# Regrouping the matmuls of each 128 by 128 weight tile: six of 260 columns become five of 280, 480 and 240

## What is computed

```python
xn = _rmsnorm(x, n_mix_pre);  proj = xn @ w_in            # 1024 -> 8192
q, fp, iv, og, lx, ly, ga, gb = jnp.split(proj, idx, axis=-1)
...
o, S_new = _hgrn2(qh, kk, vh, logf, S0, chunk)            # 8 heads, decaying state
out_a = (norm(o) * silu(og)) @ w_pa
h, h_last = _rglru(conv(lx), ...);  out_b = (gelu(ly) * h) @ w_pb
merged = sigmoid(ga) * out_a + sigmoid(gb) * out_b
x = x + _rmsnorm(merged @ w_o, n_mix_post)
gate, up = jnp.split(_rmsnorm(x, n_ffn_pre) @ w_fi, 2, axis=-1)   # 1024 -> 2 x 2816
x = x + _rmsnorm((silu(gate) * up) @ w_fo, n_ffn_post)
```

## Time and profile before

| | |
|---|---|
| three runs, median (lowest to highest) | 1102.22 us (1102.03 to 1102.48) |
| profiled execution, first to last instruction | 1098.3 us |
| its time outside that span | not recorded; the median of the runs is 3.9 us above the span |
| TensorE matmul busy / weight load busy | 96% / 94% |
| DVE busy / ACT busy | 52% / 40% |
| mean granted TensorE clock | 0.992 of 2.4 GHz |
| matmuls, of them by `ktile` (line 1223) | 8542, 7392 |

### The profile page before, as it was taken

The page is one execution under the profiler, slowest core; times in us unless marked ns, Lnnn a source line. Parts: engine busy times, 40 slices in busy tenths (PEclk is TensorE's granted clock), DMA queues, the critical chain, the costliest instruction groups (busy, mean ns, idle before and its releaser), DMA issues.

```text
span 1098.3 us, 21670 instructions
## 1 busy us (share of the span) xinstructions
PE 1055.9 (96%) x8542; PEld 1034.8 (94%) x8542; DVE 573.2 (52%) x1028; ACT 434.1 (40%) x588; POOL 2.9 (0%) x9
## 2 busy tenths in 40 slices
PE   4899999999999999999999999699999999999997
PEld 3799999999999899999999999699999999999997
DVE  2666566657656788833333333855554554422223
ACT  5434335433442888822222233652323232322222
POOL 0000000000000000000000000000000000000000
PEclk9999999999999899999999999899999999999999
DMA  5533223222332233232333244033233323233321
GB/s 155 162 90 99 79 76 98 86 76 76 94 108 60 81 93 86 78 95 81 91 95 95 88 130 135 20 97 95 80 92 95 95 82 90 67 92 94 94 76 78
DMA packets 182881, 100.36 MB, mean 91 GB/s; under 512 B 3709, under 2 KB 181378, under 8 KB 182594
## 3 DMA queue, kind: packets, MB, share of 16 engines
q1 hardware_dynamic: 164898, 90.87, 27.8%
q10 hardware_dynamic: 17792, 8.91, 2.7%
q0 software_dynamic: 160, 0.15, 0.0%
HBM read 90.79 MB, written 9.13 MB: 91 GB/s over the span
## 4 chain that ended last, share of the span: by engine, by line
PE 90%; DVE 3%; ACT 2%; issue 1%; SPq 1%; DMA 1%; DVEq 0%; ACTq 0%
PE proj L1223 78%; PE pr L1322 5%; PE pi L1371 1%; DMA raw<-in_w_in 1%; PE pr L1376 1%; PE pi L1353 1%; PE pr L1345 1%; PE pi L1414 1%; PE pr L1414 1%; PE pi L1359 0%; ACT wh L358 0%; SPq L266 0%; DVE tmp L1122 0%; DVE acts L1110 0%; DVE raw L1202 0%
## 5 line engine op out<-in xcount | busy, mean ns | idle before, releaser
L1223 PE MATMUL proj<-acts,wh 128*128 128x260 f32 x4928 | 810.7, 287 | 15.5 <-DVE acts L1110 9.2
L1223 PEld LDWEIGHTS proj<-acts,wh 128*128 128x128 f32 x4928 | 679.9, 190 | 23.7 <-DVE acts L1110 10.8
L1223 PE MATMUL proj<-acts,wl 128*128 128x260 f32 x2464 | 498.5, 284 | 0.0
L1223 PEld LDWEIGHTS proj<-acts,wl 128*128 128x128 f32 x2464 | 381.9, 190 | 0.0
L720 DVE TENSOR_TENSOR wl<-raw,wh 128x1024 fp32r<-128x1024 f32 (+2 forms) x164 | 190.8, 1163 | 278.7 <-ACT wh L358 278.6
L358 ACT ACTIVATE wh<-raw 128x1024 fp32r<-128x1024 f32 (+2 forms) x164 | 165.6, 1010 | 358.9 <-PE proj L1223 350.5
L1322 PE MATMUL pr<-tmp 128*128 128x64 f32 (+1 forms) x512 | 66.4, 272 | 3.2 <-DVE tmp L947 3.2
L1322 PEld LDWEIGHTS pr<-tmp 128*128 128x128 f32 x512 | 62.9, 192 | 4.0 <-DVE tmp L947 3.4
L805 DVE TENSOR_TENSOR tmp<-tmp 128x256 f32<-128x256 f32 x56 | 23.6, 422 | 25.5 <-PE pr L1322 25.4
L676 ACT ACTIVATE acts<-tmp 128x520 f32 (+1 forms) x21 | 13.4, 639 | 42.4 <-DVE tmp L1170 42.4
L673 ACT ACTIVATE tmp<-tmp 128x520 f32<-128x520 f32 x21 | 13.5, 641 | 40.0 <-DVE tmp L1161 40.0
(11 more groups left out here) (239 smaller groups left out, 721.0 us busy)
## 6 DMA issues: line engine op xcount, KB each, us to landing
raw<-in_w_in SPq DMA_DIRECT2D x64, 512.0 KB, 4.0
raw<-in_w_ffn_in SPq DMA_DIRECT2D x44, 512.0 KB, 3.8
raw<-in_w_ffn_out SPq DMA_DIRECT2D x16, 384.0 KB, 3.1
raw<-in_w_ffn_out SPq DMA_DIRECT2D x16, 320.0 KB, 2.9
tmp<-in_state_hgrn ACTq DMA_DIRECT2D x8, 512.0 KB, 4.1
out<-tmp ACTq DMA_DIRECT2D x8, 512.0 KB, 3.2
raw<-in_w_branch_a SPq DMA_DIRECT2D x8, 512.0 KB, 3.6
raw<-in_w_branch_b SPq DMA_DIRECT2D x8, 512.0 KB, 3.5
```

Source lines behind the costliest of these rows:

```text
L1223: o = mm(pp[par][:, hf, 0:TH], w, x[:, hf * TH:(hf + 1) * TH], start=start and n == 0, stop=stop and n == 2)
```

## The change

In `ktile` the 520 tokens are cut into a front of 280 (`TFR`) and a back of 240 (`TB`). The front, in the first bank, still gets three matmuls, of 280 columns. For the back the activation's high and low rows stand side by side in one access pattern (two runs of 240 columns), so that one matmul with the high weight streams 480 columns into the second bank; a fifth one adds the low weight times the high activation onto the first 240 of them. At the end the second bank holds two blocks of 240 that have to be added: `lift` on ACT copies the second block into SBUF (`FL`), `fold` on DVE adds it onto the first, in PSUM. `lift` stands in front of ACT's `prep` and waits for the end of the unit, `fold` stands in front of DVE's `prep`; consumers now wait for `folded`. In FFO, where four units add up, there is one pair for four units. Since front and folded back are adjacent, `proj(par)` becomes one run of 520 columns. To make room in SBUF the masks are kept once instead of four times and broadcast in `take`; one copy makes them instead of eight. In the last head's part `prep(u0 + 2, 2)` on ACT moves ahead of `pre_conv(0)`.

```diff
+TB = 240
+TFR = T - TB
+PB = 512 - TFR
...
+            def lift(par, units):
+                eng.wait_ge(E("unit_done"), units)
+                act(FL[:, par], PF[par][:, 512 + TB:512 + 2 * TB], AF.Copy).then_inc(E("lifted"), 1)
...
                 if prev:
+                    lift(1, 4 * h)
                     prep(4 * h + 1, 1)
-                    eng.wait_ge(E("unit_done"), 4 * h)
+                    eng.wait_ge(E("folded"), 4 * h)
                     eng.wait_ge(E("d_f"), h)
-                    act(halves(SIG), proj(1), AF.Sigmoid).then_inc(E("a_sg"), 1)
+                    act(SIG, proj(1), AF.Sigmoid).then_inc(E("a_sg"), 1)
...
+            lift(0, u0 + 1)
+            prep(u0 + 2, 2)
             pre_conv(0, u0)
-            prep(u0 + 2, 2)
...
+            def fold(par, units):
+                eng.wait_ge(E("lifted"), units)
+                back = PF[par][:, 512:512 + TB]
+                tt(back, back, FL[:, par], ADD).then_inc(E("folded"), 1)
...
-            for i in range(NLEV):
-                n = P if i == 0 else P // 2
-                at = 0 if i == 0 else P + (i - 1) * n
-                src = raw[:, 3].rearrange("p k n -> p (k n)")[:, at:at + n].unsqueeze(1).to_broadcast([P, NCH, n])
-                cp(mask(i).rearrange("p (c n) -> p c n", c=NCH), src).then_inc(E("m_made"), 1)
+            cp(masks[:], raw[:, 3].rearrange("p k n -> p (k n)")[:, 0:MW]).then_inc(E("m_made"), 1)
...
                 if prev:
+                    fold(1, 4 * h)
                     prep(4 * h + 1, 1)
                     level(h - 1, 4)
...
-                xh, xl = acts[:, reg[0] + koff + k], acts[:, reg[1] + koff + k]
+                ih, il = reg[0] + koff + k, reg[1] + koff + k
+                xh, xl = acts[:, ih], acts[:, il]
+                both = acts[:, bass.ds(ih, 2, step=il - ih), TFR:T]
                 a, b = wh[:, s % 2, k, :], wl[:, s % 2, k, :]
-                for n, (w, x) in enumerate(((a, xh), (a, xl), (b, xh))):
-                    for hf in range(2):
-                        o = mm(pp[par][:, hf, 0:TH], w, x[:, hf * TH:(hf + 1) * TH],
-                               start=start and n == 0, stop=stop and n == 2)
+                front, back = PF[par][:, PB:512], PF[par][:, 512:512 + TB]
+                mm(front, a, xh[:, 0:TFR], start=start, stop=False)
+                mm(front, a, xl[:, 0:TFR], start=False, stop=False)
+                mm(front, b, xh[:, 0:TFR], start=False, stop=stop)
+                mm(PF[par][:, 512:512 + 2 * TB], a, both, start=start, stop=False, skip_group_check=True)
+                o = mm(back, b, xh[:, TFR:T], start=False, stop=stop, skip_group_check=True)
```

More of the change, by code:

```diff
@@ L135, in hybrid_decoder @@
         cout = sb("cout", [P, 3 * (1 + NB), NH])
+        FL = sb("lifts", [P, 2, TB])
         pp = [ctx.enter_context(nc.psum_tensor(f"proj{i}", [P, 2, 512], F32)) for i in range(2)]
+        PF = [t[:].rearrange("p a n -> p (a n)") for t in pp]
         pr = ctx.enter_context(nc.psum_tensor("pr", [P, 2, 512], F32))
@@ L195, in mask @@
         def mask(i):
-            return masks[:, 0:TP] if i == 0 else masks[:, TP + (i - 1) * TP // 2:TP + i * TP // 2]
+            return masks[:, 0:P] if i == 0 else masks[:, P + (i - 1) * P // 2:P + i * P // 2]
         NX = CW - 1 + T + CW * NB
@@ L566, in _ @@
             eng.wait_ge(E("p_os"), NH)
+            lift(1, u0 + 2)
             squares_of_ly(0)
@@ L573, in _ @@
             out_high(h)
+            lift(0, u0 + 3)
             pre_conv(1, u0 + 2)
@@ L583, in _ @@
                     n = i * 2 + bb
+                    lift(1, u0 + 2 * bb)
                     squares_of_ly(n - 1)
@@ L588, in _ @@
                     gates(n - 1)
+                    lift(0, u0 + 2 * bb + 1)
                     prep(u0 + 2 * bb + 2, (2 * bb + 2) % 4)
@@ L593, in _ @@
                 ch.end(Q_LRU - 1)
+            lift(1, 4 * G_MIX)
             squares_of_ly(NH - 1)
@@ L598, in _ @@
             gates(NH - 1)
+            lift(0, 4 * G_MIX + 1)
             prep(4 * G_MIX + 2, 2)
@@ L654, in _ @@
                     turned_x1(j - 1)
+            lift(0, 4 * G_FFI + 1)
             prep(4 * G_FFI + 2, 2)
+            lift(1, 4 * G_FFI + 2)
             inverse_rms(1, 0)
@@ L669, in ffi @@
                     j = i * 2 + jj
+                    lift(0, u0 + 2 * jj + 1)
                     prep(u0 + 2 * jj + 2, (2 * jj + 2) % 4)
@@ L920, in hg_steps @@
                     level(h - 1, 7)
+                fold(0, 4 * h + 1)
                 prep(4 * h + 2, 2)
@@ L928, in hg_steps @@
                     chunk_states(h - 1)
+                fold(1, 4 * h + 2)
                 prep(4 * h + 3, 3)
@@ L934, in hg_steps @@
                 eng.wait_ge(E("a_sq"), h + 1)
-                tt(halves(QP), proj(1), halves(SIG), MUL).then_inc(posted(1), 1)
+                tt(QP, proj(1), SIG, MUL).then_inc(posted(1), 1)
                 if not prev:
                     softplus()
+                fold(0, 4 * h + 3)
                 prep(4 * h + 4, 0)
@@ L1018, in _ @@
             h, u0 = NH - 1, 4 * G_LRU
+            fold(1, u0)
             prep(u0 + 1, 1)
@@ L1024, in _ @@
                 level(h, i)
+            fold(0, u0 + 1)
             prep(u0 + 2, 2)
@@ L1029, in _ @@
             conv(0)
+            fold(1, u0 + 2)
             prep(u0 + 3, 3)
@@ L1036, in _ @@
             head_low(h)
+            fold(0, u0 + 3)
             prep(u0 + 4, 0)
@@ L1045, in _ @@
                     n = i * 2 + bb
+                    fold(1, u0 + 2 * bb)
                     gelu_inner(n - 1)
@@ L1051, in _ @@
                     gated(n - 1)
+                    fold(0, u0 + 2 * bb + 1)
                     prep(u0 + 2 * bb + 2, (2 * bb + 2) % 4)
@@ L1054, in _ @@
                 ch.end(Q_LRU - 1)
+            fold(1, 4 * G_MIX)
             gelu_inner(NH - 1)
@@ L1060, in _ @@
             gated(NH - 1)
+            fold(0, 4 * G_MIX + 1)
             prep(4 * G_MIX + 2, 2)
@@ L1132, in _ @@
             eng.wait_ge(E("d_x1s"), 1)
+            fold(0, 4 * G_FFI + 1)
             prep(4 * G_FFI + 2, 2)
-            eng.wait_ge(E("unit_done"), 4 * G_FFI + 2)
-            cp(halves(U(0)), proj(0)).then_inc(posted(0), 1)
-            cp(halves(U(3)), proj(1)).then_inc(posted(1), 1)
+            fold(1, 4 * G_FFI + 2)
+            eng.wait_ge(E("folded"), 4 * G_FFI + 2)
+            cp(U(0), proj(0)).then_inc(posted(0), 1)
+            cp(U(3), proj(1)).then_inc(posted(1), 1)
             prep(4 * G_FFI + 3, 3)
```

105 lines of the change are left out of this document (65 added, 40 removed).

## The result

Four runs of the changed kernel have a median of 1113.08 us (1112.41 to 1115.18), against 1102.12 for the kernel before: ratio 1.0108, interval 1.0092 to 1.0123. The change made the kernel 1.1% slower. The prediction was 1099.2 us, range 1091 to 1110.

What follows compares the result with a forecast made beforehand. TensorE's rate was taken as the bound nearly everywhere. Matmuls -10.2, heads +3.9, waiting places +3.8 and masks -0.5 sum to -3.0 us, taking 1102.2 to 1099.2 us, range 1091 to 1110.

Steps and rivals of the forecast that it cites:

- I take 11.7 ns as fixed: In `ktile`, each matmul costs 11.7 ns beyond its columns; one fewer saves 11 ns per k-tile, 10.2 us over 928.
- rival B: On TensorE nothing is won, by per-column bound or second-run restart; only losses stay, 1109.4 us; chance 0.20.
- reading (a): In `ktile`, the 11.7 ns above the ideal 108.3 are a fixed cost for each matmul.
- (b): In `ktile`, the 120.0 ns per matmul come from a stream slower than 2.4 GHz per column.
- A: Whole kernel: fixed cost per matmul, gain mostly eaten by lifts and folds at tight places; 1095 to 1103 us; chance 0.50.
- I charge nothing: In LRU, MIX, OUT, FFI and FFO, lift and fold are hidden in the unit; otherwise 0.35 us per unit.
- The heads: In the seven heads lift and fold are not hidden; net loss 0.55 us per head, 3.9 us.
- Place two: After a head's fourth unit, DVE's fold in front of level 4 delays the waiting score product by 0.36 us.
- Place one: After a head's third unit, ACT's lift before the value copy makes PE wait about 0.3 us.
- Places where PE waits: Norm behind OUT, first FFI unit, tail, last head with first LRU convolutions: lift and fold in series cost 3.8 us.
- Masks: One mask copy instead of eight lets later data arrive sooner; 0.5 us gained, up to 1.2 before a lift and fold.
- rival E: A float32r matmul with few columns runs slower, 90 to 290 ns more per k-tile; 1210 to 1460 us; chance 0.08.

Runs made afterwards that it cites:

- the blocks of 256 to 512 columns: Kernel before with blocks of 24 float32r matmuls of different sizes added behind its last work; 119 ns per matmul at 256 columns, 233 at 512.
- MIX only: Kernel before with masks kept once and the five matmuls, lift and fold in MIX alone; 1097.78 us, ratio 0.9970.
- with DVE at 94%: Changed kernel with LRU in the old form and an unused, non-waiting 240-column addition on DVE where fold stood; 1102.17 us, ratio 1.0012.
- the last traces of LRU: Changed kernel with the LRU y unit's fold moved ahead of the convolution's last tap; 1107.64 us, ratio 1.0072.

## Why the prediction was wrong

*The matmuls (wrong in size).* The step "I take 11.7 ns as fixed" failed. No run shows a fixed 11.7 ns. By the blocks of 256 to 512 columns the fixed part is 5 ns, and the rest is a stream of 0.445 ns per column, which for 240 columns comes to the floor of 112 to 113. One matmul fewer gives the 5 ns, and the second run in the 480 columns takes 2 of them back. A k-tile became 717 ns, not 709. Where PE sets the pace that is 0.7 us in MIX, 0.3 in OUT, 0.6 in FFI and 0.55 in FFO: 2.1 us, where 832 k-tiles of 11 ns were to give 9.2. This is rival B for the matmuls, which I gave 0.20. Taking reading (a) was my choice: the kernel before has `ktile` matmuls of one size only, and one size can't tell a fixed part from a slope. In the blocks 252 columns more, 512 against 260, took 114 ns, near the 116 of a stream at 120/260 ns per column (b) and not the 105 of N/2.4 (a). With so little to go by, 0.50 for A was too much.

*Where lift and fold are hidden (wrong, and the larger error).* The step "I charge nothing" for LRU failed. It looked at one chain, end of unit, lift, `wh`, `wl`, and at DVE's idle time over the whole span. It didn't follow the other chain of the same unit: end of unit, squares, `gelu_inner`, and DVE's queue up to `gelu`, which frees the PSUM for the unit two on. That chain had 0.4 us of slack in 7.5. Lift and fold in front of it would be 0.8 us, and fold waits for `conv` besides: 1.9 us in all, 1.5 of them beyond the slack. Cost 9.3 us, plus 1.6 in MIX's first units. None of the cases held it: rival B, with nothing won, still ended at 1109.4. B's sum had a slip as well: its 7.2 us kept the 0.2 us per head that other k-tiles were to win, which B denies; without them it is 8.6 us and 1110.8, still without LRU. In MIX, OUT, FFI and FFO the charge of nothing was nearly right: 0.0 to 0.7 us per stage by the kernel without lift and fold.

*The heads (right in the sum, by luck in part).* Net 0.55 us per head was forecast; 0.42 is the mean of the seven and 0.44 the fifth. Place two cost 0.36, as forecast. Place one cost 0.16, not 0.3 (from the score product before it to this one 2.49 us, against 2.33 before), the fold in front of level 8 nothing that shows, and the other k-tiles gave 0.1, not 0.2.

*Places where PE waits (right).* Norm and first FFI unit 1.5 forecast; 1.5 against the profile of before, 1.2 against others with the old form there. Tail 0.8, measured 0.84. Last head and first convolution 1.5, measured 1.15.

*Masks (right in sign, too small).* 0.5 forecast, 1.7 to 4.2 measured by the timed runs. The bound was 1.2; what gave more isn't settled, since the first stage goes with the place where the clock falls: a wait of 2.9 us stood in front of the score product in one trace with the new masks (MIX only) and 1.1 in another (masks alone).

*The sum.* Forecast -10.2 + 3.9 + 3.8 - 0.5 = -3.0. By stages: -2.1 in MIX, OUT, FFI and FFO, +2.9 heads, +3.5 at the waits, -1.9 in the first stage, and +10.9 for LRU's last 12 units with what they pass on to MIX (9.3 + 1.6): +13.3 of the 13.4 us between the spans. Matmuls that give 8 us less, and LRU's 11 us that nobody had counted, are more than the whole error; 1.0 came back in the heads and 1.4 in the first stage. Between the spans the error is 16.4 us, 1111.7 against 1095.3. Against the medians it is 13.9, since the profiled execution of before was 2.1 below its median run and that of after 0.4 above.

## What to carry to other kernels

Before you charge nothing for an operation put behind a unit, take the stage with the busiest helpers by itself and follow each consumer of that unit to the point where it frees the buffer; compare its end with the end of the unit between. A share of busy time doesn't answer it: with DVE at 94% nothing was lost, while two operations of 0.4 us, one of them waiting for its engine besides, in front of a chain with 0.4 us of slack cost 1.5 us per round. And measure the rate at two sizes before pricing a regrouping: excess time over the ideal can be slope, not a fixed part.

## What the runs showed of the hardware

A `float32r` matmul of 128 rows, each with its own load, takes 113 ns at 128, 192 and 240 columns and from 256 to 512 columns 5 ns plus 0.445 ns per column (119 at 256, 233 at 512), at a granted clock of 1.00. Two runs of 240 columns in one matmul took 219 ns, one run of 480 took 217. At 128, 192 and 240 columns nothing was slower than these 113 ns, so rival E falls.

The granted clock of TensorE was 1.00 or 0.50, and in every trace it was at the lower one for stretches of 3.4 us and longer in LRU and in front of FFI, where TensorE waits, and in all but one in the first head. With 3.4 us more at the lower level MIX's first pair took 1.4 us longer (the last traces of LRU) (17.0 against 15.6) and the first four LRU units 1.6 (42.95 against 41.35). In MIX a wait of 1.9 us, in place of 1.2, stood in front of the fall; that the longer wait brought it on isn't shown.
